# A hybrid decoder trunk on one core: rounding steps, SSD groups and GDN taps in other places

## The chip, the cores and the metric

The kernel runs on one core of a Trainium2 chip. The metric is the device time of one execution in microseconds, the median of several runs. TensorE (PE in the profile) multiplies matrices, with PEld for its weight loads; VectorE is DVE, ScalarE is ACT, GpSimd is POOL, SyncE is SP. Each engine works through its own queue of instructions in order, and the engines meet only at semaphores.

## The reference

A two-layer trunk on 256 prompt tokens and 8 x 4 sample tokens, 288 columns together, width 2048:

```python
for i in range(DEPTH):                     # DEPTH = 2
    hn = rmsnorm(h, norm_w[i])
    mix = gdn_mixer(...) if i % 2 == 0 else ssd_mixer(...)
    h = h + mix
    e = rmsnorm(p_i @ w_proj, norm_w)      # ple_add
    h = h + e * sigmoid(h @ w_gate)
y = rmsnorm(h, final_norm_w)
```

The GDN mixer (gated DeltaNet, 16 query/key heads of 128, 32 value heads) projects hn to q, k, v and z, convolves q, k, v over 4 positions, applies silu, and runs the delta rule in chunks for the prompt (with a triangular inverse per chunk) and token by token for the samples. The SSD mixer (Mamba-2, 8 groups of 8 heads of 64, state 128) projects to z, x, B, C and dt, convolves, and runs chunked state space duality for the prompt and a recurrence for the samples. Each mixer multiplies its branch with silu(z), normalises and projects back to 2048. Outputs are y and all states and convolution caches, all float32.

## The kernel before

**Precision and the weight stream.** The weights are read in halves of a tile: 128 x 1024 float32 into one of four places of `ring` by SyncE (L303 to L312). ScalarE rounds a half to `wh` (`upper`, L796 to L801; `ahead` rounds the two halves of one tile), GpSimd computes the rest `wl` = ring - wh in four instructions of 128 x 256 (`lower`, L327). The input is likewise split into `xh` (ScalarE, `split_x`, L811) and `xl` (VectorE, `lower_x`, L1345). `project` (L340) is one of eight slots of a tile of 128 output rows: two pieces of 128 inner rows, for each three matmuls with 288 columns, w_h x_h, w_h x_l and w_l x_h (L350, L351, L352). A slot is thus 6 matmuls, a tile 48. Its first slot and its fifth wait for `wl_ready`. A place of wh may be written again when TensorE has finished the half three before it (`half_done`). `project_pair` (L361) runs the first two tiles of a stage interleaved, so that each new piece of x is used at once for both.

**Stages.** The norm of x and a few GDN tiles of preparation; the GDN loop over 16 heads, the last one written out; the output projection (two `dense` parts of 16 tiles, the second fed by `split_x`); `ple` (the projection of p and the gate stage: sixteen tiles, each followed by sigmoid, a product and a sum on VectorE, and a square); the norm before SSD (`normed_x`, `norm_x`); the SSD loop over 8 groups, the last one written out; output projection and `ple` again, and the final norm.

**Mixing.** In the GDN and SSD loops TensorE's queue is written out by hand: slot e of the group's projection, then the small matmuls of the current group that hang at e (`gdn_mix`, `ssd_mix`; `gdn_ready` holds a slot's wait ahead of the projection). GDN has slots 0 to 47 a head, SSD 80 a group. ScalarE's and VectorE's orders are written out beside it: in the SSD loop `took(k)` takes tile k out of PSUM and rounds tile k + 2; `decays(c)` makes the decay matrix of chunk c from eight Relu and one Exp; `conv_silu` follows the convolution. VectorE's `do.link` makes an instruction wait for the one before it where it needs its result.

**What touches the change.** In GDN the inverse is built in six levels; at each, VectorE multiplies a result with a mask (`mask_p`, L1527), TensorE multiplies, VectorE subtracts (`less_q`, L1537, L1540). Between them lie the taps of the value convolution (`v_tap`, L1514 to L1523), and at levels 3 and 4 two sample steps (`g_bs`, L1554, and `g_es`). In SSD TensorE's groups hang at slots 21, 25, 27, 29, 31, 35, 39, 42, 46, 57 and 72: transposes at 21, the first chunk's state matmul (L717) at 25, which needs `s_xd` of VectorE's `decayed(0)` (L1812), the sample read at 27 and so on. In `ple`, ScalarE rounds `te + 1` and `te + 2` after split_x, then waits for the sum of squares, takes the root, and goes on with `gate` and `square`; VectorE follows the root with a reciprocal (L1721), sixteen scalings (L1724), and then one `gated` step for each tile (L1732, L1733), whose result `hnew` ScalarE's later gates and squares wait for.

Of the kernel before, what the change touches and what calls it, by code (L numbers as in the profile page):

```python
# [19 lines left out]
ALU = mybir.AluOpType  # L20
# [3 lines left out]
P = 128  # L24
# [58 lines left out]
G_DVE_LINKS, S_DVE_LINKS = 17, 36  # L83
# [52 lines left out]
def build(nc, weights, x_in, p_in, prm_in, cst_in, gpack, spack, gstate, sstate,  # L136
          y_out, gconv_out, sconv_out, gst_p, gst_s, sst_p, sst_s,
          g_rows, s_rows, h_spill, G_DVE, G_ACT, S_DVE, S_ACT):
    with ExitStack() as ctx:  # L139
# [199 lines left out]
        def _(pe):  # L339
# [72 lines left out]
            def gdn_ready(m, e):  # L412
# [5 lines left out]
                if e == 14:  # L418
                    pe.wait_ge(S("g_bs"), m + 1)
                if e == 26:  # L420
                    pe.wait_ge(S("g_sample_act"), m * 4 + SMP_ACT["vnds"])

            def gdn_mix(m, e, more):
# [56 lines left out]
                if e == 14:  # L480
# [35 lines left out]
                if e == 22:  # L516
# [5 lines left out]
                if e == 23:  # L522
# [9 lines left out]
                if e == 26:  # L532
# [151 lines left out]
            def ssd_mix(m, e):  # L684

                if e == 21:
# [10 lines left out]
                if e == 27:  # L697
# [8 lines left out]
                if e == 29:  # L706
# [7 lines left out]
                if e == 25:  # L714
                    pe.wait_ge(S("s_xd"), m * 2 + 1)
                    pe.wait_ge(S("s_btc"), m + 1)
                    pe.matmul(psA[:, :], sBT[:, 0, :], sa["XD"], start=True, stop=True).then_inc(S("s_s"), 1)  # L717
                for c in range(NC):
                    if e == (31, 39)[c]:
                        pe.wait_ge(S("s_w"), m * 2 + c + 1)  # L720
                        for i in range(SX):
                            for j in range(2):
                                mm = pe.matmul((psB, psC)[c][HD * j:HD * j + HD, i * P:(i + 1) * P],
                                               sX[:, c, 2 * i + j, :], sDT[:, 2 * i + j, :], start=True, stop=True)
                        mm.then_inc(S("s_y"), 1)
                if e == 35:
                    pe.wait_ge(S("s_s1"), m + 1)
                    for i in range(SX):
# [1372 lines left out]
```

## Time and profile before

| what | us |
|---|---|
| median of 3 runs | 2591.24 (2588.82 to 2592.79) |
| the profiled execution, its own time | 2590.68 |
| its span | 2588.9 |
| TensorE busy | 2439.7 (94%) |
| GpSimd busy | 1734.7 (67%) |
| VectorE busy | 1491.2 (58%) |
| ScalarE busy | 1181.6 (46%) |

The span goes from the first to the last instruction that the profiler recorded; the execution's own time is 1.8 us more. Busy times are of one execution. A matmul's duration in the timeline is longer than the distance between two starts, since matmuls overlap, so what one costs is read from the distance of starts.

### The profile page before, as it was taken

What the parts mean: (1) busy time and instruction counts of PE and PEld (TensorE: products, weight loads), DVE (VectorE), ACT (ScalarE), POOL (GpSimd) and SP (SyncE); (2) the same over time, 40 slices, a digit from 0 to 9 for tenths busy, and PEclk for the clock granted to TensorE, in tenths of its full rate; (3) what the DMA queues carried; (4) which work ended last, traced back from release to release, by engine and by line L of the source; (5) the groups of instructions that cost most, each with busy time, mean ns of one, the idle gap of its engine ahead of it and who ended that gap; (6) DMA issues with size and microseconds to landing.
All of it is one profiled execution on the core that took longest, in us unless ns stands there. A gap on an engine that the chain in (4) does not pass through costs nothing.

```text
span 2588.9 us, 58121 instructions
## 1 busy us (share of the span) xinstructions
PE 2439.7 (94%) x21088; PEld 2262.6 (87%) x21088; DVE 1491.2 (58%) x2978; ACT 1181.6 (46%) x2116; POOL 1734.7 (67%) x2236
## 2 busy tenths in 40 slices
PE   5999999999999999999998989999999999999887
PEld 4889888888888888889998879988898888899887
DVE  7555665555656556562114457888888888611434
ACT  4444444444444444443334346454545455433433
POOL 4455555555555555556797768877887777889776
PEclk9999999999999999999999989999999999999989
DMA  5344444334333343434443336655576546454433
GB/s 193 137 147 140 145 139 147 123 134 139 127 129 129 139 145 139 139 133 169 147 163 135 136 140 228 230 182 184 199 237 207 184 169 220 176 175 156 141 123 125
DMA packets 126772, 410.83 MB, mean 159 GB/s; under 512 B 21345, under 2 KB 37985, under 8 KB 122113
## 3 DMA queue, kind: packets, MB, share of 16 engines
q1 hardware_dynamic: 81216, 295.75, 33.0%
q10 hardware_dynamic: 45504, 114.38, 13.1%
q8 instruction: 35, 0.57, 0.1%
q14 instruction: 17, 0.13, 0.0%
HBM read 363.47 MB, written 46.61 MB: 158 GB/s over the span
## 4 chain that ended last, share of the span: by engine, by line
POOL 59%; issue 37%; PE 3%; POOLq 1%; DVE 0%; ACT 0%; DVEq 0%; ACTq 0%
POOL wl L327 59%; PE psj L350 1%; PE psj L352 1%; PE psj L351 1%; POOLq L331 0%; POOLq L325 0%; DVE h L1940 0%; DVE arena L1938 0%; ACT L1150 0%; POOLq L327 0%; ACT arena L1125 0%; PE psA L374 0%; ACT arena L1333 0%; DVE arena L1410 0%; DVEq L139 0%
## 5 line engine op out<-in xcount | busy, mean ns | idle before, releaser
L327 POOL TENSOR_TENSOR wl<-ring,wh 128x256 fp32r<-128x256 f32 x2232 | 1734.5, 811 | 832.5 <-ACT wh L801 829.9
L350 PE MATMUL psj<-xh,wh 128*128 128x288 f32 x4400 | 1376.3, 313 | 74.9 <-POOL wl L327 33.7
L351 PE MATMUL psj<-xl,wh 128*128 128x288 f32 x4400 | 1312.7, 298 | 0.0
L352 PE MATMUL psj<-xh,wl 128*128 128x288 f32 x4400 | 1307.5, 297 | 0.0
L350 PEld LDWEIGHTS psj<-xh,wh 128*128 128x128 f32 x4400 | 838.0, 190 | 143.7 <-issue 62.9
L351 PEld LDWEIGHTS psj<-xl,wh 128*128 128x128 f32 x4400 | 840.8, 191 | 5.4 <-issue 4.4
L352 PEld LDWEIGHTS psj<-xh,wl 128*128 128x128 f32 x4400 | 841.9, 191 | 0.0
L801 ACT ACTIVATE wh<-ring 128x1024 fp32r<-128x1024 f32 x558 | 575.2, 1056 | 530.6 <-PE psj L352 464.3
L872 ACT ACTIVATE arena<-psj 128x256 f32<-128x256 f32 x112 | 42.6, 381 | 265.9 <-PE psj L352 265.9
L1766 DVE SCALAR_TENSOR_TENSOR arena<-arena 128x256 f32<-128x256 f32 x144 | 124.2, 902 | 2.6
L1699 DVE TENSOR_TENSOR h<-h,psj 128x288 f32 x32 | 14.5, 454 | 173.7 <-PE psj L352 173.7
L1518 DVE SCALAR_TENSOR_TENSOR arena<-arena 128x256 f32<-128x256 f32 x192 | 100.4, 563 | 0.0
L1732 DVE TENSOR_TENSOR arena<-Y,arena 128x288 f32<-128x288 f32 x32 | 21.6, 674 | 120.2 <-ACT arena L1119 120.2
L1689 DVE COPY Y<-psj 128x288 f32 x22 | 10.1, 458 | 131.5 <-PE psj L352 131.5
L1439 DVE SCALAR_TENSOR_TENSOR arena<-arena 128x256 f32<-128x256 f32 x192 | 83.8, 494 | 1.2
L1527 DVE TENSOR_TENSOR arena<-psC,cst 128x256 f32<-128x256 f32 x96 | 40.6, 423 | 56.1 <-PE psC L379 54.2
L379 PEld LDWEIGHTS psC<-arena 128*64 128x64 f32 x1536 | 52.8, 138 | 15.9 <-issue 15.9
L379 PE MATMUL psC<-arena 128*64 128x64 f32 x1536 | 66.1, 228 | 0.0
L1886 DVE TENSOR_TENSOR h<-h,arena 128x512 f32<-128x512 f32 x64 | 64.9, 1013 | 0.2
L1540 DVE SCALAR_TENSOR_TENSOR arena<-psE,cst,arena 128x256 f32<-128x256 f32 x96 | 46.4, 483 | 30.8 <-PE psE L379 27.9
L1537 DVE TENSOR_TENSOR arena<-arena,psA 128x256 f32<-128x256 f32 x80 | 33.7, 422 | 51.4 <-PE psA L379 48.1
L1119 ACT ACTIVATE arena<-psj 128x288 f32<-128x288 f32 x32 | 13.1, 409 | 107.5 <-PE psj L352 107.5
(345 smaller groups left out, 2895.0 us busy)
## 6 DMA issues: line engine op xcount, KB each, us to landing
ring<-weights_d SPq DMA_DIRECT2D x558, 512.0 KB, 3.3
h<-gstate_d ACTq DMA_DIRECT2D x16, 1024.0 KB, 4.8
gst_s_d<-h ACTq DMA_DIRECT2D x16, 1024.0 KB, 4.6
h<-sstate_d ACTq DMA_DIRECT2D x32, 512.0 KB, 5.4
sst_s_d<-h ACTq DMA_DIRECT2D x32, 512.0 KB, 6.0
arena<-g_rows_d ACTq DMA_DIRECT2D x16, 864.0 KB, 4.2
arena<-s_rows_d ACTq DMA_DIRECT2D x8, 1152.0 KB, 8.0
h_spill_d<-h ACTq DMA_DIRECT2D x2, 2304.0 KB, 8.0
```

Source lines behind the costliest of these rows:

```text
L327: ins = pool.tensor_tensor(wl[:, s, n:n + 2], ring[:, s, n:n + 2], wh[:, s, n:n + 2].bitcast(F32), ALU.subtract)
L350: pe.matmul(out, w_h, xh[:, kt, :], start=(kt == 0), stop=False)
L351: pe.matmul(out, w_h, xl[:, kt, :], start=False, stop=False)
L352: mm = pe.matmul(out, w_l, xh[:, kt, :], start=False, stop=(kt == KT - 1))
L379: mm = pe.matmul(bank[r:r + 64, cols], lhsT[:, r:r + 64], rhs, start=True, stop=True)
L801: act.activation(wh[:, hc % 4], ring[:, hc % 4], ACT.Copy).then_inc(wh_ready, 1)
L872: return lambda bank: (act.activation(U[:, i, UP:UC], bank[:, 0:SEQ], ACT.Copy), act.activation(U[:, i, US:UW], bank[:, SEQ:T], ACT.Copy))[1]
L1439: ins = dve.scalar_tensor_tensor(out, src, tap(i, j), out, ALU.mult, ALU.add)
L1518: ins = dve.scalar_tensor_tensor(out, gU[:, 2 + i, at:at + b - a], gpc_tap[1][:, i, j:j + 1], out, ALU.mult, ALU.add)
L1540: dve.scalar_tensor_tensor(E, packed(psE[:, 0:2 * P], lv), cst[:, K_BM, K_ROW + lv:K_ROW + lv + 1], E, ALU.mult, ALU.add).then_inc(S("g_de ...
L1766: ins = dve.scalar_tensor_tensor(out, src, w, out, ALU.mult, ALU.add)
L1886: do.link(dve.tensor_tensor(sS[:, b], sS[:, b], bc(sEGb[:, :, b], 2, HD), ALU.mult))
```

## The change

- SyncE loads the first and third quarter of x and the constants; ScalarE loads the second and fourth quarter and prm, and no longer waits for prm before it issues the loads of gpack.
- `split_x` and `normed_x` can round one half of the next tile before their wait for `half_done`, and one in the middle of their sixteen pieces. The dense stages use both; the gate stage the one in the middle, and a half of its first tile at i = 13 of the squares. After the root ScalarE rounds tile by tile between the first gates, and the squares come two gates behind instead of one.
- SSD: groups at 20, 32, 34, 44, 49, 59 and 72 instead of eleven. The state matmul of the first chunk goes from slot 25 to 32, with the sample read; slot 34 holds the off-diagonal product, the second state, the sample transposes and the first chunk's y; slot 44 the second chunk's y and the transposes of 42. ScalarE's silu of the sample rows goes behind `decays(0)`, the copy of the first state goes before the copy of the sample read, and VectorE's steps for the second chunk go ahead of the sample steps.
- GDN: `v_tap` does either the prompt or the sample part; they stand one by one between masks and subtractions and end behind mask 4. The wait for `g_bs` goes from slot 14 to 15, the groups of 22, 26 and 28 go to 23 and 27. The cache rows `gco` are copied later with a semaphore `g_co` of their own, and the silu of the value rows comes before the DMA of the cache.

The core of the diff:

```diff
-            for n in range(4):
+            for n in (0, 2):
                 sp.dma_start(h[:, 4 * n:4 * n + 4, :], x_in[:, 4 * n:4 * n + 4, :]).then_inc(S(f"x_in{n}"), 16)
-                if n == 0:
-                    sp.dma_start(cst[:, :, :], cst_in).then_inc(c_in, 16)
-                    sp.dma_start(prm[:, :], prm_in).then_inc(S("prm_in"), 16)
+            sp.dma_start(cst[:, :, :], cst_in).then_inc(c_in, 16)
             for s in range(4):
...
-                if e == 14:
+                if e == 15:
                     pe.wait_ge(S("g_bs"), m + 1)
-                if e == 26:
+                if e == 27:
                     pe.wait_ge(S("g_sample_act"), m * 4 + SMP_ACT["vnds"])
...
-                if e == 22:
+                if e == 23:
                     pe.wait_ge(S("g_es"), m + 1)
                     pe.wait_ge(S("g_rss"), m + 1)
...
-                if e == 23:
                     pe.wait_ge(S("g_vnd"), m * 2 + 1)
...
-                if e == 26:
+                if e == 27:
+                    pe.wait_ge(S("g_rhs"), m + 1)
+                    new_values(1)
...
-                if e == 27:
-                    pe.wait_ge(S("g_rhs"), m + 1)
-                    new_values(1)
-                if e == 28 and more:
-                    gdn_norm(m + 1)
+                    if more:
+                        gdn_norm(m + 1)
                 if e == 29:
...
-                if e == 21:
+                if e == 20:
...
+                def chunk_state(c):
+                    pe.wait_ge(S("s_xd"), m * 2 + c + 1)
+                    pe.matmul(psA[:, :], sBT[:, c, :], sa["XD"], start=True, stop=True).then_inc(S("s_s"), 1)
+
+                def chunk_y(c):
+                    pe.wait_ge(S("s_w"), m * 2 + c + 1)
...
+                if e == 32:
+                    pe.wait_ge(S("s_btc"), m + 1)
+                    chunk_state(0)
                     pe.wait_ge(S("s_pr"), m + 1)
                     col_sum(psF[:, 0:NPAIR], sPR)
...
-                if e == 29:
+                if e == 34:
+                    pe.wait_ge(S("s_s1"), m + 1)
...
+                    chunk_state(1)
                     pe.wait_ge(S("s_roc"), m + 1)
...
-                if e == 25:
-                if e == 35:
...
-                    pe.wait_ge(S("s_xd"), m * 2 + 2)
-                    pe.matmul(psA[:, :], sBT[:, 1, :], sa["XD"], start=True, stop=True).then_inc(S("s_s"), 1)
-                if e == 42:
+                    chunk_y(0)
+                if e == 44:
+                    chunk_y(1)
                     pe.wait_ge(S("s_xe"), m + 1)
...
                 for r in range(2):
-                    if e == (46, 57)[r]:
+                    if e == (49, 59)[r]:
...
-            def split_x(src, n, t0):
-
+            def split_x(src, n, t0, first=False, second=False):
+
+                if first:
+                    upper(0, 0, 2 * t0 + 2)
                 if t0:
                     act.wait_ge(half_done, 2 * t0)
                 for kt in range(n):
+                    if second and kt == n // 2:
+                        upper(0, 0, 2 * t0 + 3)
                     act.activation(xh[:, kt, :], src(kt), ACT.Copy).then_inc(xh_ready, 1)
 
-            def normed_x(base, t0, t_next):
+            def normed_x(base, t0):
 
                 act.wait_ge(S("hss"), base // KT + 1)
                 act.activation(dRS, psA[:, 0:T], ACT.Sqrt, bias=eps_c, scale=1.0 / D_MODEL) \
                     .then_inc(S("n_root"), 1)
                 if t0:
+                    upper(0, 0, 2 * t0 + 2)
                     act.wait_ge(half_done, 2 * t0)
                 else:
                     ahead(0, 0, 0)
                 for kt in range(KT):
+                    if kt == 3 and not t0:
+                        upper(0, 0, 2)
                     if kt == KT // 2:
-                        ahead(0, 0, t_next)
+                        upper(0, 0, 2 * t0 + 3)
                     act.wait_ge(S("xn"), base + kt + 1)
                     act.activation(xh[:, kt, :], dTM[:, kt % 2, :], ACT.Copy).then_inc(xh_ready, 1)
...
+            for n in (1, 3):
+                act.dma_start(h[:, 4 * n:4 * n + 4, :], x_in[:, 4 * n:4 * n + 4, :]).then_inc(S(f"x_in{n}"), 16)
+            act.dma_start(prm[:, :], prm_in).then_inc(S("prm_in"), 16)
             act.wait_ge(S("konst"), 1)
             act.activation(small[:, 7:8], eps_c, ACT.Sqrt)
-            act.wait_ge(S("prm_in"), 16)
...
-            normed_x(0, 0, 1)
+            normed_x(0, 0)
             act.dma_start(h_spill, h[:, :, :]).then_inc(S("spill"), 16)
+            act.wait_ge(S("prm_in"), 16)
...
                 act.wait_ge(S("g_convv"), m + 1)
+                act.activation(gCR[:, 2:4, :], gCR[:, 2:4, :], ACT.Silu).then_inc(S("g_cv"), 1)
+                if full:
+                    g_load_v(m + 1)
+                else:
+                    split_x(lambda kt: Y[:, kt, :], KT, T_O1)
...
+                act.wait_ge(S("g_co"), m + 1)
                 act.dma_start(gconv_out[m, 1], gco[:, 2:4, :]).then_inc(S("g_cv_out"), 16)
-                if full:
-                    g_load_v(m + 1)
-                act.activation(gCR[:, 2:4, :], gCR[:, 2:4, :], ACT.Silu).then_inc(S("g_cv"), 1)
-                if not full:
-                    split_x(lambda kt: Y[:, kt, :], KT, T_O1)
                 act.wait_ge(S("g_tokv"), m + 1)
...
             def dense(t0, src):
-                split_x(src, KT, t0)
-                ahead(0, 0, t0 + 1)
+                split_x(src, KT, t0, True, True)
                 with act.Fori(0, KT // 2 - 1) as i:
                     for k in range(2):
                         ahead(i, 2, t0 + 2 + k)
...
                 for i in range(KT):
                     if i == 7:
                         ahead(0, 0, te)
+                    if i == 13:
+                        upper(0, 0, 2 * te + 2)
                     act.wait_ge(took_dve, td + i + 1)
                     act.activation(eq[:, i, :], eb[:, i, :], ACT.Square).then_inc(S("esq"), 1)
 
...
                         .then_inc(S("hsq"), 1)
 
                 act.wait_ge(took_dve, td)
-                split_x(lambda kt: h[:, kt, :], KT, te)
-                ahead(0, 0, te + 1)
+                split_x(lambda kt: h[:, kt, :], KT, te, second=True)
                 ahead(0, 0, te + 2)
                 act.wait_ge(S("ess"), hq // KT)
                 act.activation(dRE, psB[:, 0:T], ACT.Sqrt, bias=eps_c, scale=1.0 / D_MODEL) \
                     .then_inc(S("e_root"), 1)
                 gate(0, 0)
+                ahead(0, 0, te + 3)
                 gate(0, 1)
-                square(0, 0)
-                with act.Fori(0, KT // 2 - 2) as i:
+                for k in range(2):
+                    ahead(0, 0, te + 4 + k)
+                    gate(0, 2 + k)
+                    square(0, k)
+                with act.Fori(0, KT // 2 - 3) as i:
                     for k in range(2):
-                        ahead(i, 2, te + 3 + k)
-                        gate(i, 2 + k)
-                        square(i, 1 + k)
-                ahead(0, 0, te + KT - 1)
-                gate(0, KT - 2)
-                square(0, KT - 3)
+                        ahead(i, 2, te + 6 + k)
+                        gate(i, 4 + k)
+                        square(i, 2 + k)
                 if not end:
                     ahead(0, 0, te + KT)
+                gate(0, KT - 2)
+                square(0, KT - 4)
                 gate(0, KT - 1)
+                square(0, KT - 3)
...
-            normed_x(16, T_SPRO, T_SPRO + 1)
+            normed_x(16, T_SPRO)
...
-                def took(k):
+                def took(k, between=None):
 
                     tile_wait(mt, per, t0 + k)
                     bank = psj[(t0 + k) % 2]
...
                         act.activation(sZS[:, z_of[k], :], bank[:, 0:T], ACT.Silu).then_inc(took_act, 1)
                     if not full and k == SX - 1:
                         split_x(lambda kt: Y[:, kt, :], KT, T_O2)
+                    if between is not None:
+                        between()
                     ahead(mt, per, t0 + k + 2)
...
                 took(0)
                 conv_silu(m, 1)
-                took(1)
-                conv_silu(m, 2).then_inc(S("s_cv"), 1)
-                act.wait_ge(S("s_sconv"), m + 1)
-                act.activation(sCV[:, :, SEQ:T], sCV[:, :, SEQ:T], ACT.Silu).then_inc(S("s_scv"), 1)
+                took(1, lambda: conv_silu(m, 2).then_inc(S("s_cv"), 1))
...
                 act.activation(sa["DEC"], sa["DEC"], ACT.Exp).then_inc(S("s_dec"), 1)
                 decays(0)
+                act.wait_ge(S("s_sconv"), m + 1)
+                act.activation(sCV[:, :, SEQ:T], sCV[:, :, SEQ:T], ACT.Silu).then_inc(S("s_scv"), 1)
                 if full:
                     act.wait_ge(S("s_cv"), m + 1)
                     s_load_pack(m + 1)
                 took(2)
+                if not full:
+                    took(3)
+                act.wait_ge(S("s_s"), m * 2 + 1)
+                act.activation(sS1, psA[:, :], ACT.Copy).then_inc(S("s_s1"), 1)
                 act.wait_ge(S("s_ro"), m + 1)
                 act.activation(sRO, psE[:, :], ACT.Copy).then_inc(S("s_roc"), 1)
-                act.wait_ge(S("s_s"), m * 2 + 1)
-                act.activation(sS1, psA[:, :], ACT.Copy).then_inc(S("s_s1"), 1)
-                took(3)
+                if full:
+                    took(3)
                 act.wait_ge(S("s_y"), m * 2 + 1)
...
-                def v_tap(i, j):
-
...
+                def v_tap(i, j, part):
+
+                    a, b, at = ((0, SEQ, j), (SEQ, T, UC + DEC_B * j))[part]
+                    out = gCR[:, 2 + i, a:b]
+                    return dve.scalar_tensor_tensor(out, gU[:, 2 + i, at:at + b - a], gpc_tap[1][:, i, j:j + 1],
+                                                    out, ALU.mult, ALU.add)
...
+                mask_p(0)
+                do.link(v_tap(0, 0, 0))
+                less_q(0)
+                do.link(v_tap(0, 0, 1))
+                mask_p(1)
+                do.link(v_tap(1, 0, 0))
+                less_q(1)
+                v_tap(1, 0, 1)
+                do.link(v_tap(0, 1, 1))
+                mask_p(2)
+                do.link(v_tap(0, 1, 0))
+                less_q(2)
+                do.link(v_tap(1, 1, 0))
+                mask_p(3)
+                dve.wait_ge(S("g_sample_pe"), m * 6 + SMP_PE["sqs"])
...
+                do.link(v_tap(0, 2, 0))
+                less_q(3)
+                v_tap(1, 2, 0)
+                do.link(v_tap(1, 1, 1))
+                mask_p(4)
+                v_tap(0, 2, 1)
+                v_tap(1, 2, 1).then_inc(S("g_convv"), 1)
+                dve.wait_ge(S("g_sample_pe"), m * 6 + SMP_PE["esp"])
...
+                if not full:
+                    lower_x(lambda kt: Y[:, kt, :], KT, X0["oa1"])
+                less_q(4)
                 dve.tensor_copy(gco[:, 2:4, 0:PRE], gU[:, 2:4, UC - PRE:UC])
-                dve.tensor_copy(gco[:, 2:4, PRE:CW], gU[:, 2:4, UW - PRE * DEC_B:UW])
-                for lv in range(6):
-                    mask_p(lv)
-                    if lv < PRE:
-                        v_tap(0, lv)
...
+                do.link(dve.tensor_tensor(sCB[:, :, :], psD[:, 0:2 * P].rearrange("p (c t) -> p c t", c=NC),
+                                  bc(cst[:, K_INC, :], 1, NC), ALU.mult))
                 dve.wait_ge(S("s_scv"), m + 1)
...
-                dve.wait_ge(S("s_cb"), m + 1)
                 dve.wait_ge(S("s_dt"), m * 2 + 1)
                 dve.tensor_tensor(sDT[:, :, :], sDT[:, :, :], bc(sCB[:, 0, :], 1, HPG), ALU.mult).then_inc(S("s_w"), 1)
+                if last:
+                    lower_x(lambda kt: Y[:, kt, :], KT, X0["oa2"])
                 dve.wait_ge(S("s_s"), m * 2 + 1)
                 decayed(1)
 
                 dve.tensor_tensor(sXS[:, :, :], sCV[:, 2:6, SEQ:T], sRP[:, :, 192:224], ALU.mult)
+                dve.wait_ge(S("s_off"), m + 1)
+                y1 = sYT[:, :, CH:SEQ]
+                do.link(dve.tensor_tensor(y1, psD[:, :].rearrange("p (i t) -> p i t", i=SX), sRP[:, :, 32:160],
+                                          ALU.mult))
+                dve.wait_ge(S("s_s"), m * 2 + 2)
+                s1 = sS1.rearrange("p (h d) -> p h d", h=HPG)
+                do.link(dve.tensor_tensor(s1, s1, bc(sEGc, 2, HD), ALU.mult))
+                dve.tensor_tensor(sS1, sS1, psA[:, :], ALU.add).then_inc(S("s_s2"), 1)
...
-                if last:
-                    lower_x(lambda kt: Y[:, kt, :], KT, X0["oa2"])
...
```

## Rows read from the trace of the kernel before

**Rows 1.** The page's busy table, and its costliest group on GpSimd.

```profile
PE 2439.7 (94%) x21088; PEld 2262.6 (87%) x21088; DVE 1491.2 (58%) x2978; ACT 1181.6 (46%) x2116; POOL 1734.7 (67%) x2236
...
L327 POOL TENSOR_TENSOR wl<-ring,wh 128x256 fp32r<-128x256 f32 x2232 | 1734.5, 811 | 832.5 <-ACT wh L801 829.9
```

**Rows 2.** TensorE's waits: us in total, times, longest us.

```profile
PE psj L350 <- POOL wl L327: 33.7, 8, 6.3
...
PE psA L717 <- DVE arena L1812: 18.2, 7, 2.6
...
PE psA L379 <- DVE arena L1527: 3.2, 14, 0.2
```

**Rows 3.** Windows: stretch, us, busy by engine, PEclk, DMA share, GB/s.

```profile
1300.00:1380.00 80.00, 80.00 (x602) 80.00 (x601) 13.67 (x25) 26.49 (x26) 73.14 (x103) 1.00 0.49 171
1288.00:1293.00 5.00, 5.00 (x23) 5.00 (x23) 0.00 (x0) 0.00 (x0) 4.96 (x8) 0.50 0.61 208
```

**Rows 4.** Timeline, one GDN head: start us, us, engine, line, [idle before].

```profile
388.29 0.40 PE L350 MATMUL psj<-xh,wh 128*128 128x288 f32 x1 [0.64 <-DVE arena L1554]
...
411.70 0.40 PE L350 MATMUL psj<-xh,wh 128*128 128x288 f32 x1
...
412.59 0.61 PE L508 MATMUL psC<-arena 128*128 128x128 f32 x4
```

**Rows 5.** Timeline, TensorE at the stages' first waits for wl.

```profile
1287.52 0.61 PE L350 MATMUL psj<-xh,wh 128*128 128x288 f32 x1 [4.21 <-POOL wl L327]
...
1416.66 0.61 PE L350 MATMUL psj<-xh,wh 128*128 128x288 f32 x1 [5.83 <-POOL wl L327]
...
1440.39 0.61 PE L350 MATMUL psj<-xh,wh 128*128 128x288 f32 x1 [6.28 <-POOL wl L327]
```

**Rows 6.** Windows at half clock behind the six waits, first and sum.

```profile
1286.40:1293.20 6.80, 5.68 (x23) 5.68 (x24) 0.00 (x0) 0.00 (x0) 6.61 (x10) 0.50 0.45 154
...
sum 34.00, PE 25.03 PEld 25.04 DVE 4.28 ACT 6.19 POOL 33.14; mean PE 4.17 PEld 4.17 DVE 0.71 ACT 1.03 POOL 5.52
```

**Rows 7.** Timeline, first gate stage, VectorE and GpSimd.

```profile
1425.64 1.95 DVE L1721 RECIPROCAL arena<-arena 128x288 f32<-128x288 f32 x1 [10.29 <-ACT arena L1133]
1427.62 6.96 DVE L1724 SCALAR_TENSOR_TENSOR Y<-Y,prm,arena 128x288 f32<-128x288 f32 x16
...
1437.06 11.89 POOL L327 TENSOR_TENSOR wl<-ring,wh 128x256 fp32r<-128x256 f32 x16 [10.03 <-ACT wh L801]
```

**Rows 8.** Timeline, VectorE in the norm before SSD.

```profile
1545.76 0.87 DVE L1358 SCALAR_TENSOR_TENSOR arena<-h,prm,arena 128x288 f32<-128x288 f32 x1
1546.55 0.99 DVE L1364 TENSOR_TENSOR xl<-arena,xh 128x288 fp32r<-128x288 f32 x1
...
1549.42 0.52 DVE L1358 SCALAR_TENSOR_TENSOR arena<-h,prm,arena 128x288 f32<-128x288 f32 x1
1549.86 0.45 DVE L1364 TENSOR_TENSOR xl<-arena,xh 128x288 fp32r<-128x288 f32 x1
```

**Rows 9.** Timeline, an SSD group (TensorE, ScalarE) and the last one's end.

```profile
1692.24 0.37 ACT L1264 ACTIVATE arena<-psA 128x256 f32<-128x256 f32 x1
1692.63 1.28 ACT L1266 ACT_TABLE_LOAD   x1
...
1693.91 1.13 PE L717 MATMUL psA<-arena 128*128 128x512 f32 x2 [2.60 <-DVE arena L1812]
...
1694.55 2.43 ACT L1244 ACTIVATE arena<-arena 128x128 f32<-128x128 f32 x8
1697.02 1.06 ACT L1248 ACTIVATE arena<-arena 128x1024 f32<-128x1024 f32 x1
...
2208.91 0.58 PE L350 MATMUL psj<-xh,wh 128*128 128x288 f32 x1 [4.03 <-DVE xl L1349]
```

**Rows 10.** The start: ScalarE's first squares, and x's four transfers.

```profile
7.53 1.11 ACT L865 ACTIVATE arena<-h 128x288 f32<-128x288 f32 x3 [5.28 <-DMA prm<-prm_in_d]
...
DMA to landing us min/median/max: 3.9/6.7/8.2
```

More of the change, by code:

```diff
@@ L479, in gdn_mix @@
                     mm.then_inc(S("g_sample_pe"), 1)
-                if e == 14:
+                if e == 15:
                     for j in range(2):
@@ L696, in ssd_mix @@
                     mm.then_inc(S("s_tok"), 1)
-                if e == 27:
+                def chunk_state(c):
[3 more added lines that the diff above has]
+                    pe.wait_ge(S("s_w"), m * 2 + c + 1)
+                    for i in range(SX):
+                        for j in range(2):
+                            mm = pe.matmul((psB, psC)[c][HD * j:HD * j + HD, i * P:(i + 1) * P],
+                                           sX[:, c, 2 * i + j, :], sDT[:, 2 * i + j, :], start=True, stop=True)
+                    mm.then_inc(S("s_y"), 1)
+                if e == 32:
+                    pe.wait_ge(S("s_btc"), m + 1)
+                    chunk_state(0)
                     pe.wait_ge(S("s_pr"), m + 1)
@@ L705, in ssd_mix @@
                     mm.then_inc(S("s_ro"), 1)
-                if e == 29:
+                if e == 34:
+                    pe.wait_ge(S("s_s1"), m + 1)
+                    for i in range(SX):
+                        mm = pe.matmul(psD[:, i * P:(i + 1) * P], sS1[:, i * P:(i + 1) * P],
+                                       sCV[:, 1, CH:2 * CH], start=True, stop=True)
+                    mm.then_inc(S("s_off"), 1)
+                    chunk_state(1)
                     pe.wait_ge(S("s_roc"), m + 1)
@@ L713, in ssd_mix @@
                     mm.then_inc(S("s_smp"), 1)
-                if e == 25:
[L715 to L725, printed above, removed]
-                if e == 35:
-                    pe.wait_ge(S("s_s1"), m + 1)
-                    for i in range(SX):
-                        mm = pe.matmul(psD[:, i * P:(i + 1) * P], sS1[:, i * P:(i + 1) * P],
-                                       sCV[:, 1, CH:2 * CH], start=True, stop=True)
-                    mm.then_inc(S("s_off"), 1)
-                    pe.wait_ge(S("s_xd"), m * 2 + 2)
-                    pe.matmul(psA[:, :], sBT[:, 1, :], sa["XD"], start=True, stop=True).then_inc(S("s_s"), 1)
-                if e == 42:
+                    chunk_y(0)
+                if e == 44:
+                    chunk_y(1)
                     pe.wait_ge(S("s_xe"), m + 1)
@@ L1512, in gdn_body @@
                 ins.then_inc(S("g_mk"), 1)
-                def v_tap(i, j):
-                    for a, b, at in ((0, SEQ, j), (SEQ, T, UC + DEC_B * j)):
-                        out = gCR[:, 2 + i, a:b]
-                        ins = dve.scalar_tensor_tensor(out, gU[:, 2 + i, at:at + b - a], gpc_tap[1][:, i, j:j + 1],
-                                                       out, ALU.mult, ALU.add)
-                    if (i, j) == (1, PRE - 1):
-                        ins.then_inc(S("g_convv"), 1)
-                    else:
-                        do.link(ins)
+                def v_tap(i, j, part):
[3 more added lines that the diff above has]
+                                                    out, ALU.mult, ALU.add)
                 def mask_p(lv):
@@ new lines, in gdn_body @@
+                dve.tensor_tensor(gBS[:, :, :], bc(ident[0:NS, 0:NS], 1, 2),
+                                  psD[0:NS, 256:256 + 2 * NS].rearrange("p (j t) -> p j t", j=2), ALU.add) \
+                    .then_inc(S("g_bs"), 1)
+                do.link(v_tap(0, 2, 0))
[6 more added lines that the diff above has]
+                dve.wait_ge(S("g_sample_pe"), m * 6 + SMP_PE["esp"])
@@ L1568, in qk_taps @@
+                mask_p(5)
+                less_q(5)
                 def qk_taps(js):
```

34 lines of the change are left out of this document (6 added, 28 removed).

## Prediction

> **What bounds the kernel now.** I read the busy table of the page first: TensorE is busy 94% of the span. GpSimd, busy 67%, is named often as the one that others wait for, but of its own 832.5 idle us 829.9 end with ScalarE's rounding [rows 1]: it is a link between ScalarE and TensorE, not the bound. So TensorE's own queue sets the end, and time can come from four things only: waits in it, half clock, the step from projections to group work and back, and less work. The arithmetic stays the same.
>
> Next I read TensorE's waits [rows 2]. 33.7 us in 8 waits are for wl, up to 6.3 us each; they stand at the begin of the output stages. 18.2 us are seven waits of L717 for DVE L1812 in the SSD loop; 3.2 us are fourteen of L379 for L1527 in the GDN loop.
>
> Last I read the price of a projection matmul: in 80 us of a dense stage 602 start, 0.133 us each, at the granted clock 1.00 (2.4 GHz); in 5 us behind a wait 23 start, 0.22 to 0.24 us each, at 0.50 (1.2 GHz) [rows 3]. A long wait is paid twice.
>
> **GDN loop (16 heads).** (a) The wait for g_bs (L1554) before slot 14's projection is 0.64 us [rows 4]; at slot 15, a slot of about 0.9 us later, g_bs is there. (b) Today two taps run between a mask and the subtraction behind it, or the other way, and TensorE waits for it: 3.2/14 = 0.23 us per head [rows 2], and as much again, an estimate, in the projection run that starts inside the same lateness. A piece alone fits under a projection slot. I take 0.4 us. (c) Three group slots disappear (22, 26, 28). A run of six projection matmuls between two groups takes 0.89 us (411.70 to 412.59) instead of 6 x 0.133 = 0.80 [rows 3, 4]; I take 0.1 to 0.2 each, 0.12, so 0.36. Sum 1.4 us, times 15 = 21.0; bounds 1.0 and 1.8 per head, 15 to 27. New waits: ScalarE waits for the silu of the value rows until their taps end, now behind mask 4, and for g_co; behind the last it has only g_tokv's work, which comes later. In the last head, where split_x of the output stage stands behind that silu, I book 0.4 us won. Sum 21.4.
>
> **Output stages (dense, twice).** ScalarE today makes sixteen xh pieces and only then rounds the next half; GpSimd's four subtractions end 4.21 us too late for TensorE [rows 5]. With one half rounded before the wait and one in the middle, wl is there. What is late next is xh piece 8, behind the rounding in the middle, and DVE's xl pieces, slowed by GpSimd: 0.5 us. Gain 2 x (4.21 - 0.5) = 7.4; bounds 5 and 8.4.
>
> **Gate stages (twice).** The waits are 5.83 and 6.28 us, and the same in the second layer, 24.2 in all [rows 5]. What comes instead, each time: the square behind the early rounding, 0.4; xl pieces beside GpSimd, 0.8; e_sum's wait for DVE's sums, 0.3. Then the second wait does not go entirely. ScalarE's gate(0, 2) waits for the first new h, and that follows DVE's sixteen scalings, 6.96 us today, 0.44 each, with GpSimd idle for 10.03 us around them [rows 7]. GpSimd will now work through all of them. The nearest rows are DVE's in the norm before SSD, beside GpSimd and without it: the scaling L1358 takes 0.87 against 0.52, the subtraction L1364 0.99 against 0.45 [rows 8]. At 0.8 us each, sixteen are 12.8 us, so the first new h comes some 15 us behind the root (reciprocal 1.95), while TensorE has three tiles of 48 x 0.133 = 6.4 us, of which the root takes the first part: I work out 3.2 us of wait before the fifth tile. At the end a third square stands behind the last gate: 0.5. Gain 24.2 - 2 x (0.4 + 0.8 + 0.3 + 3.2 + 0.5) = 13.8; bounds 4 (scalings at 1.1) and 22 (at 0.45).
>
> **Half clock behind these six waits.** TensorE works 25.03 us at 0.50 behind them [rows 6], each matmul at 0.24 instead of 0.133: 11.1 us are lost. All of it goes but 1.1 us for each new wait in the gate stages: 8.9; bounds 6 and 11. Output and gate stages together: 7.4 + 13.8 + 8.9 = 30.1.
>
> The Trainium skill (SBUF — State Buffer, SBUF: two separate sides) speaks against this step: an instruction of VectorE with two SBUF inputs and one of GpSimd exclude each other for whole instructions. By it every scaling would wait out one GpSimd instruction of 0.7 us, 16 x 1.15 = 18.4 us, and each gate stage would lose another 5.6. The rows agree that they slow each other, by a factor of 1.7 to 2.2.
>
> **SSD loop (8 groups).** DVE's chain is continuous up to L1812, so slot 25's state matmul waits 2.60 us in the iterations from the second on [rows 9]. In slot 32 its input is long there. Gone per iteration: 2.60; four group slots, 0.5; what the wait costs in the clock behind it, 0.9 (an estimate from [rows 6]: 4.2 us at half clock, of which 1.9 are lost, follow each wait of 4 to 6 us); small waits at L709 and L723 together, 0.9, an estimate. 4.9 us. But slots 21 to 31 hold no group now, and TensorE is at slot 32, the first of tile 4, after eleven slots of 0.80 us, 8.9 us behind the transposes. Tile 4's weights are rounded by took(2), and this stays behind decays(0) in ScalarE's order and now also behind the sample silu. Its chain from the transposes: copy 0.35, table load 1.28, three exps 0.6, decays 2.43 + 1.06 [rows 9], then a second table load 1.28, silu 0.4, take_u 0.45, rounding 1.0, GpSimd's four 2.8, and 0.6 for handing over: 12.2 us. New wait: 3.3 us in every iteration, also in the first. Today TensorE comes there 5 us later and nobody waits. 4.9 - 3.3 = 1.6; six times 9.8, the first one 2.3 lost, half clock 1 lost. Sum 6.5; bounds -8 (also 2.2 us at slot 44 if DVE's linked sample steps run at their speed beside GpSimd) and 30 (no new wait). The last group: today 2.6 [rows 2] and 4.03 us of waits [rows 9] and one between them; 2.5 of half clock (by [rows 6]). Then 3.3 at slot 32, 0.6 for its xl, and 2.1 at slot 34, where the second state waits behind sixteen xl pieces. Gain 4.8; bounds 0 and 9.
>
> **Norm before SSD.** ScalarE rounds in two single steps and one earlier, so less of norm_x runs beside GpSimd at the upper prices of [rows 8]: 1.5 us; bounds 0 and 3.
>
> **Start.** The squares start at 7.53, ended by prm's landing; x's four transfers land 3.9 to 8.2 us after their issues [rows 10], so a quarter takes 1.43 us and the first was there at 0.8 + 3.9 = 4.7. Over two queues the first two quarters land together at about 6.1, so 1.4 us are won. The third half begun at piece 3 keeps TensorE busy sooner: 1.6. Sum 3.0; bounds 1 and 5. ScalarE's three DMA issues ahead of its table load, and the gpack issues behind it, lie under the wait for x.
>
> **Sum.** 21.4 + 30.1 + 6.5 + 4.8 + 1.5 + 3.0 = 67.3 us. The profiled execution took 2590.68, 1.8 us more than its span and 0.6 less than the median of the runs; 2590.7 - 67.3 = 2523.4, and I predict 2523.
>
> **Rivals.** *No new wait at slot 32* (0.12): ScalarE's chain is shorter than I add up, or TensorE comes later. Speaks for it that GpSimd is idle there; against it the order of ScalarE's queue. 8 x 3.3 = 26 less: 2497. *Earlier rounding only moves the wait* (0.15): the slowdown between GpSimd and DVE gives the stages' gain back, the scalings take 1.15 us each and the xl pieces in the dense stages run out too: 30.1 becomes 13: 2540. *The finer taps miss* (0.06): another DVE instruction is late in the inversion and (b) and part of (a) come back, 0.8 x 16: 2536. *Slower than before* (0.05): slot 32's wait is worse. ScalarE's rounding of tile 4 is now behind s_sconv, the end of DVE's sample convolution; each us that this comes later than ScalarE asks for it is one of TensorE's wait, eight times. It decides at a wait of 3.3 + 67/8 = 11.7 us: 2592 and more. *The edits do little* because other waits stand behind each: 0.02, 2589. My forecast has 0.60.
>
> **Numbers.** The bounds' half widths, added as squares, give about 14 us around the forecast; reaching to the rivals on both sides: 2498 to 2550. Faster by over 0.2% (5 us, about what a measurement of this kernel can tell from no change): 0.93; within: 0.02; slower: 0.05.
>
> **What would show it.** GDN: no wait for L1554, a head's period 1.4 us shorter. Dense: the 4.2 us waits for wl under 0.6, no half clock there. Gate: the first wait gone, a second of 2 to 4 us released by ScalarE's gate or the first new h, DVE's scalings at 0.7 to 0.9 us. SSD: no wait at L717, one of 3 us for wl at L350, a second table load before took(2). Start: squares from about 6. The prediction is wrong if the wait at slot 32 is absent or grows past 5 us, or if the scalings keep 0.44 us.

## Result and profile after

The changed kernel takes 2576.56 us (median of five runs; 2574.27 to 2577.94), the kernel before 2591.24 (also of five): a ratio of 0.9944, 95% interval 0.993 to 0.9959. It is faster by 0.56%, 14.7 us, where 68 us were forecast and 2550 was the end of the range.

I split both traces at the first projection matmul of each stage. A positive number is time won by the stage; the sum is the difference of the two spans, 2588.9 and 2575.0.

| stage | forecast us | measured us |
|---|---|---|
| start and first tiles | 3.0 | 1.7 |
| GDN loop and last head | 21.4 | 20.0 |
| output stages, both | 11.4 | 9.3 |
| gate stages, both | 18.7 | 12.6 |
| norm before SSD | 1.5 | 0.6 |
| SSD loop, groups 1 to 7 | 6.5 | -21.7 |
| last SSD group, to the second dense stage | 4.8 | -8.5 |

(The gate row is -1.31 for the projection of p and 6.24 for the gate tiles in the first layer, -1.39 and 9.06 in the second, the last with the final norm in it.) Outside SSD the gate stages are 6.1 us off, no other stage more than 2.1. "Last SSD group" runs from its first tile through the first half of the output projection. The SSD edits lost 30.2 us: the section from the loop's first tile to the second dense stage was 735.3 us and is 765.5.

The busy table and GpSimd's group of the changed kernel, against [rows 1]:

```profile
PE 2450.3 (95%) x21088; PEld 2267.1 (88%) x21088; DVE 1465.1 (57%) x2978; ACT 1199.8 (47%) x2130; POOL 1761.8 (68%) x2236
...
L325 POOL TENSOR_TENSOR wl<-ring,wh 128x256 fp32r<-128x256 f32 x2232 | 1761.6, 822 | 787.9 <-ACT wh L800 785.3
```

TensorE does the same 21088 matmuls, but is busy for 10.6 us longer, and its mean granted clock is 0.974 where it was 0.980: that is the first hint that the loss is not in waits alone. ScalarE has fourteen instructions more, all table loads: eight ahead of the sample silu, and seven more ahead of the Exp of `decays(1)`, less one elsewhere.

TensorE's waits after (us in total, times, longest), against [rows 2]:

```profile
PE psj L348 <- POOL wl L325: 32.5, 10, 4.5
...
PE psj L348 <- ACT arena L1130: 6.9, 2, 3.7
...
PE psA L696 <- DVE arena L1841: 3.2, 1, 3.2
```

The sum for wl has hardly changed, 32.5 for 33.7, and this is a trap: the waits are other ones. The four of the gate stages and two of the dense stages [rows 5] are gone; eight in SSD's slot 32 stand in their place, one a group, and two short ones are left. L717's seven waits are gone as well, as are those for L1554 and L1527.

Slot 32 of the second SSD group in the changed kernel, TensorE's timeline and then ScalarE's:

```profile
1675.93 0.61 PE L348 MATMUL psj<-xh,wh 128*128 128x288 f32 x1 [3.83 <-POOL wl L325]
...
1677.54 1.91 PE L696 MATMUL psA<-arena 128*128 128x512 f32 x2
1679.24 0.56 PE L372 MATMUL psF<-arena,cst 128*128 128x80 f32 x2
```

```profile
1668.15 1.06 ACT L1264 ACTIVATE arena<-arena 128x1024 f32<-128x1024 f32 x1
1668.29 0.34 ACTq L1195 DMA_DIRECT2D arena<-spack_d  x1
1669.23 1.28 ACT L1285 ACT_TABLE_LOAD   x1
1670.52 0.37 ACT L1285 ACTIVATE arena<-arena 128x192 f32<-128x192 f32 x1
1670.80 0.36 ACT L881 ACTIVATE arena<-psj 128x256 f32<-128x256 f32 x1
1671.07 0.19 ACT L882 ACTIVATE arena<-psj 128x32 f32<-128x32 f32 x1
1671.14 2.00 ACT L800 ACTIVATE wh<-ring 128x1024 fp32r<-128x1024 f32 x2
```

This is the chain that I added up: decays, table load, silu, take_u, rounding. TensorE stopped at 1672.1 and went on at 1675.93. What I had not added stands behind it: from the start of L696's two matmuls to that of L372 it is 1.70 us.

Windows of the changed kernel at half clock around slot 32 of the eight SSD groups (columns as in [rows 3]; first two, last and sum):

```profile
1589.50:1596.30 6.80, 5.95 (x22) 3.21 (x26) 0.90 (x2) 0.60 (x1) 3.54 (x6) 0.50 0.46 154
1674.80:1681.60 6.80, 5.67 (x22) 3.18 (x26) 0.89 (x2) 0.60 (x1) 3.82 (x6) 0.50 0.45 154
...
2186.80:2193.60 6.80, 4.78 (x18) 2.97 (x22) 6.80 (x9) 6.53 (x16) 6.76 (x9) 0.50 0.25 85
sum 54.60, PE 43.91 PEld 24.58 DVE 13.06 ACT 10.71 POOL 34.27; mean PE 5.49 PEld 3.07 DVE 1.63 ACT 1.34 POOL 4.28
```

TensorE works 43.91 us at 1.2 GHz there, and the last group has more behind it: the granted clock is 0.50 again from 2200.5 to 2210.7. Before, the 2.60 us waits were followed by half clock in four of seven groups, for 13.05 us of work in all:

```profile
1777.90:1781.30 3.40, 3.40 (x18) 2.96 (x20) 0.51 (x2) 3.37 (x11) 0.00 (x0) 0.50 0.09 22
...
sum 13.60, PE 13.05 PEld 10.40 DVE 4.19 ACT 13.48 POOL 0.00; mean PE 3.26 PEld 2.60 DVE 1.05 ACT 3.37 POOL 0.00
```

### The profile page after: what moved, and what is told of

It is laid out like the page before. It is cut to its first block, busy times and chain, and to the rows that moved or that the text cites. A ratio compares the mean times of both kernels' runs of the same rounds, so it can differ in the third digit from the quotient of the medians.

```text
span 2575.0 us, 58133 instructions
## 1 busy us (share of the span) xinstructions
PE 2450.3 (95%) x21088; PEld 2267.1 (88%) x21088; DVE 1465.1 (57%) x2978; ACT 1199.8 (47%) x2130; POOL 1761.8 (68%) x2236
## 4 chain that ended last, share of the span: by engine, by line
POOL 49%; issue 32%; PE 14%; DVE 3%; ACT 1%; POOLq 1%; ACTq 0%; DVEq 0%
POOL wl L325 49%; PE psj L348 5%; PE psj L350 4%; PE psj L349 4%; DVE xl L1367 1%; DVE Y L1753 1%; POOLq L329 0%; DVE h L1968 0%; POOLq L323 0%; DVE h L1914 0%; ACT wh L800 0%; PE psA L696 0%; PE psA L747 0%; PE psj L659 0%; ACT xh L819 0%
## 5 line engine op out<-in xcount | busy, mean ns | idle before, releaser
L325 POOL TENSOR_TENSOR wl<-ring,wh 128x256 fp32r<-128x256 f32 x2232 | 1761.6, 822 | 787.9 <-ACT wh L800 785.3
L348 PE MATMUL psj<-xh,wh 128*128 128x288 f32 x4400 | 1365.1, 310 | 75.1 <-POOL wl L325 32.5
L1795 DVE SCALAR_TENSOR_TENSOR arena<-arena 128x256 f32<-128x256 f32 x144 | 123.6, 897 | 2.6
L1728 DVE TENSOR_TENSOR h<-h,psj 128x288 f32 x32 | 14.5, 454 | 154.9 <-PE psj L350 154.9
L1428 DVE TENSOR_TENSOR arena<-arena 128x288 f32<-128x288 f32 x45 | 22.8, 506 | 109.3 <-ACT arena L1136 101.9
L1457 DVE SCALAR_TENSOR_TENSOR arena<-arena 128x256 f32<-128x256 f32 x192 | 83.7, 494 | 1.2
L1536 DVE SCALAR_TENSOR_TENSOR arena<-arena 128x256 f32<-128x256 f32 (+1 forms) x192 | 69.0, 381 | 0.0
L1551 DVE TENSOR_TENSOR arena<-arena,psA 128x256 f32<-128x256 f32 x80 | 33.7, 421 | 62.1 <-PE psA L377 62.1
L1554 DVE SCALAR_TENSOR_TENSOR arena<-psE,cst,arena 128x256 f32<-128x256 f32 x96 | 46.5, 484 | 31.4 <-PE psE L377 27.8
L377 PE MATMUL psE<-arena 128*64 128x64 f32 x1536 | 61.9, 223 | 0.0
```

The lines of the kernel that those rows point to most:

```text
L325: ins = pool.tensor_tensor(wl[:, s, n:n + 2], ring[:, s, n:n + 2], wh[:, s, n:n + 2].bitcast(F32), ALU.subtract)
L348: pe.matmul(out, w_h, xh[:, kt, :], start=(kt == 0), stop=False)
L377: mm = pe.matmul(bank[r:r + 64, cols], lhsT[:, r:r + 64], rhs, start=True, stop=True)
L1457: ins = dve.scalar_tensor_tensor(out, src, tap(i, j), out, ALU.mult, ALU.add)
L1536: return dve.scalar_tensor_tensor(out, gU[:, 2 + i, at:at + b - a], gpc_tap[1][:, i, j:j + 1], out, ALU.mult, ALU.add)
L1554: dve.scalar_tensor_tensor(E, packed(psE[:, 0:2 * P], lv), cst[:, K_BM, K_ROW + lv:K_ROW + lv + 1], E, ALU.mult, ALU.add).then_inc(S("g_de ...
```

## Experiments

Ratios are to the kernel before, with 95% intervals. What a run gains against the changed kernel is the difference of the two medians.

**The change without its SSD part, and the SSD part alone.** In the first the groups, ScalarE's order and VectorE's order of the SSD loop are those of before; in the second they alone are new.

> The changed kernel with TensorE's groups, ScalarE's and VectorE's order of the SSD loop as before (s_cb stays a link, for the number of semaphores). Theory: the SSD edits cost what the section from the loop's first tile to the second dense stage shows, 765.5 against 735.3 us, so 30 us come back: 2546 us, a loop period of 83.1 and again a 2.6 us wait at the first state matmul. Rival (the rest of the change lengthens the SSD section through its changed start, the roundings in took or the norm): 2565 or more, and a loop period that stays near 85.

> The kernel before with the SSD edits alone. Theory: 30 us slower than before, 2621 us, a wait for wl of 3.8 us in slot 32 in all eight groups, a loop period of 85.4. Rival (the loss is an interaction with the other edits): within 10 us of before.

2547.37 us, 0.9833 (0.9816 to 0.9849), and 2619.19 us, 1.0112 (1.0095 to 1.0129). By themselves the SSD edits cost 28 us (30 were expected), taken out they give 29 back. They are additive to the rest, so the cause is inside them. In the second run the waits for wl double in number:

```profile
PE psj L350 <- POOL wl L327: 65.1, 16, 6.3
```

**Tile 4 rounded early.**

```diff
                 act.activation(sa["BT"], psA[:, 0:2 * P], ACT.Copy).then_inc(S("s_btc"), 1)
+                ahead(mt, per, t0 + 4)
+                act.wait_ge(S("s_sconv"), m + 1)
+                act.activation(sCV[:, :, SEQ:T], sCV[:, :, SEQ:T], ACT.Silu).then_inc(S("s_scv"), 1)
+                took(2, rounded=True)
...
                 decays(0)
-                act.wait_ge(S("s_sconv"), m + 1)
-                act.activation(sCV[:, :, SEQ:T], sCV[:, :, SEQ:T], ACT.Silu).then_inc(S("s_scv"), 1)
...
-                took(2)
```

> The changed kernel, with ScalarE's two roundings of tile 4 ahead of the sample silu, the exps and decays(0), and the silu ahead of the exps (one table load fewer). Theory (the loss is ScalarE's order: 3.8 us of wait and 2.5 us of half clock on the float32 group matmuls behind it): no wait for wl in slot 32, the two state and read groups at 0.85 and 1.7 instead of 1.7 and 2.7 us, loop period 79 to 80, 2526 to 2535 us. Rival (the merged groups ask too early for VectorE's work anyway): a wait for s_pr or s_w of 2 to 4 us takes its place, period above 83, above 2555 us.

2522.75 us, 0.9736 (0.9719 to 0.9752): 54 us less than the changed kernel and 3 less than the range expected, with the same groups on TensorE. The edit moves more than the two roundings: the silu and take_u of tile 2 go ahead of the exps too, and one table load of each group falls away. A group takes 78.7 to 79.5 us; it was 82.8 to 83.3 before and is 85.3 to 85.5 in the changed kernel. The same matmuls in this run:

```profile
1665.50 1.02 PE L696 MATMUL psA<-arena 128*128 128x512 f32 x2
1667.06 0.45 PE L372 MATMUL psF<-arena,cst 128*128 128x80 f32 x2 [0.54 <-DVE arena L1860]
```

and two groups later:

```profile
1824.47 1.02 PE L696 MATMUL psA<-arena 128*128 128x512 f32 x2
1825.33 0.34 PE L372 MATMUL psF<-arena,cst 128*128 128x80 f32 x2
```

The wait for wl is gone, and from the start of L696 to that of L372 it is 0.86 us, not 1.70, in the five groups without a wait between them. So the merged groups, fed in time, win 4.4 us a group on average, close to the 4.9 that I had summed; ScalarE's order took it away. The rival, that the merged groups ask too early for VectorE's work, shows as 0.54 us in two groups, each 0.8 us longer than the others. The section of the last group is not mended: 160.0 us, where the kernel before took 157.7; a wait of 4.55 us for the first xl pieces stands there.

**The roundings between decays and silu.** Here only `ahead(mt, per, t0 + 4)` moves, to a place ahead of the second table load, so that short waits stay.

> The changed kernel with only the order of two ScalarE steps in the SSD loop turned round: decays(0), then the two roundings of tile 4, then the second table load with the sample silu, where the silu stood first. It shortens the 3.83 us wait in slot 32 by the 1.95 us of table load and silu and keeps it as a wait. The silu is 2 us later, so VectorE's s_pr is late for the same slot by 1 to 1.5 us. Theory (each long wait brings 3 us of half clock in the float32 group matmuls behind it, and short ones do not): clock back in most groups, period 81.5 to 82.5, 2545 to 2556 us. Rival (the loss is the wait's own length and nothing else): the gain is only what the waits lose, 8 x 0.5 to 8 x 1.9, 2561 to 2572 us.

2544.61 us, 0.9822 (0.9807 to 0.9837). Its waits:

```profile
PE psF L372 <- DVE arena L1860: 8.8, 7, 1.3
PE psj L348 <- ACT arena L882: 8.8, 8, 1.2
```

(L882 is the second copy of take_u, which empties the PSUM bank that the projection of slot 32 writes; it now comes behind the silu.) The window at the same place:

```profile
1666.40:1673.20 6.80, 5.54 (x36) 3.20 (x37) 5.06 (x8) 1.85 (x5) 2.50 (x4) 1.00 0.43 154
```

The waits of a group are 1.17 + 1.26 = 2.43 us, 1.40 less than 3.83, but its period is 81.64, 3.72 less than 85.36. The other 2.3 us are the clock: it stays at 1.00 through both waits of all seven groups, and TensorE starts 36 matmuls in 6.8 us where it was 22. The rival (only the wait counts) gave 2561 to 2572 and is out.

**Four scalings ahead.**

```diff
-                for i in range(KT):
-                    ins = dve.scalar_tensor_tensor(eb[:, i, :], eb[:, i, :], prm[:, wc + i:wc + i + 1], dRE,
-                                                   ALU.mult, ALU.mult)
-                do.link(ins)
+                scaled(0, 4)
...
                 gated(0, 0)
                 gated(0, 1)
+                scaled(4, KT)
```

> The changed kernel, with four of VectorE's sixteen scalings in each gate stage ahead of the first two gated steps and twelve behind them. Theory (the 3.68 us wait for ScalarE's gate comes from the sixteen scalings of 0.92 us beside GpSimd): the wait and the 2.3 us of half clock behind it go in both stages, 11 to 12 us: 2565 us. Rival (the first wait at the stage, for xl, takes it up, or the later h costs the same in another gate): under 4 us, 2573 or more.

2565.31 us, 0.9906 (0.9889 to 0.9922), 11.3 us less than the changed kernel. L1130 has left TensorE's waits: its two, 3.68 + 3.26 = 6.94 us in the changed kernel, are gone. The other 4 us I put down to the clock: of the four stretches of the gate stages at 0.50, one is left. In the changed kernel VectorE, GpSimd and TensorE show what it was:

```profile
1396.50 14.55 DVE L1753 SCALAR_TENSOR_TENSOR Y<-Y,prm,arena 128x288 f32<-128x288 f32 x16
...
1397.22 14.40 POOL L325 TENSOR_TENSOR wl<-ring,wh 128x256 fp32r<-128x256 f32 x16 [0.18 <-ACT wh L800]
...
1413.07 0.60 PE L348 MATMUL psj<-xh,wh 128*128 128x288 f32 x1 [3.68 <-ACT arena L1130]
```

Sixteen scalings in 14.55 us, 0.91 each against 0.44 with GpSimd idle [rows 7]. In this run four of them take 2.78 us and the first new h is there at 1402.1, not at 1412.4.

**The xl pieces of the last group in two parts.** Six ahead of `decayed(1)`, ten behind it.

> The changed kernel with one edit in the last SSD group: VectorE makes six of the output projection's sixteen xl pieces ahead of decayed(1) and ten behind it. Theory (the second state in slot 34 waits 3.21 us because all sixteen pieces, 13.99 us at 0.87 each, stand ahead of it): no wait there, 3 to 4 us off the section, 2573 us. Rival (VectorE is the bound of that whole section, so a later wait for take_out's copies grows by as much): section unchanged within 1 us, 2576 us.

2567.92 us, 0.9907 (0.9893 to 0.9921), 8.6 us less than the changed kernel; the section itself gains 6.1, where 3 to 4 were expected. VectorE in the changed kernel, and in this run:

```profile
2186.26 13.99 DVE L1367 TENSOR_TENSOR xl<-Y,xh 128x288 fp32r<-128x288 f32 x16
```

```profile
2185.81 5.49 DVE L1367 TENSOR_TENSOR xl<-Y,xh 128x288 fp32r<-128x288 f32 x6
2191.90 0.69 DVE L1841 TENSOR_TENSOR arena<-arena 128x512 f32<-128x512 f32 x1 [0.59 <-PE psA L696]
2192.51 8.06 DVE L1367 TENSOR_TENSOR xl<-Y,xh 128x288 fp32r<-128x288 f32 x10
```

The 3.21 us wait of L696 is gone; a wait of 1.46 us comes at the second y group (L702), so the rival is right in part. The rest of the 6.1 is clock again: behind the 3.21 us wait the changed kernel worked at half clock, here it does not. The spans of the two profiled executions differ by 6.7 us; what the medians have beyond that lies within their intervals, and I leave it open.

**The GDN part in two.** VectorE's and ScalarE's half alone, and TensorE's half alone.

> The kernel before with VectorE's and ScalarE's part of the GDN edits alone (taps in pieces, g_co, silu ahead of the DMA); TensorE's groups and waits as before. By the prediction's terms: 0.4 us a head from the pieces, the 0.64 us wait for g_bs stays: period 68.9, 2585 us. Rival (the finer taps miss): period 69.3, 2591 us.

> The kernel before with TensorE's part of the GDN edits alone: g_bs at slot 15, groups of 22, 26 and 28 merged. By the prediction's terms: 0.64 and 0.36 us a head, period 68.3, 2576 us. If merging saves nothing: period 68.7, 2581 us.

2583.53 us, 0.9972 (0.9961 to 0.9984), and 2577.34 us, 0.9948 (0.9933 to 0.9963). A head takes 69.34 us before, 68.87 with the taps, 68.61 to 68.65 with the slots, and 68.17 with both. So the taps give 0.47 (forecast 0.4) and the slots 0.71 (forecast 1.0); together they are additive. The 0.71 is the wait for g_bs alone: slots 13 to 15 take 5.54 us for 6.23, while slots 22 and 23 (3.23 before and after) and 26 to 29 (6.98 and 6.99), where the groups were merged, take what they took. The 0.36 us booked for three group slots fewer did not come.

**The edits together.**

> The changed kernel with both edits of the two runs before: tile 4 rounded early, and four scalings ahead of the first gated steps. If the two act on different waits their gains add up: 2522.75 - (2576.6 - 2565.3) = 2511.5 us. If one of them used cover of the other: 2516 or more.

> The changed kernel with all three edits: tile 4 rounded early, four scalings ahead, the xl pieces in two parts. In the run with the first two the second state of the last group waited for nothing (its slot comes later there, behind a 4.55 us wait for the first xl pieces), so the third edit has no wait to remove: 2513 to 2515 us. If it adds its 6 to 8 us all the same: 2507.

2513.74 us, 0.9702 (0.9689 to 0.9715), and 2515.4 us, 0.9707 (0.9694 to 0.972). The first two edits act on different waits and nearly add up: the second still gives 9.0 of its 11.3 us. The third has nothing to take away once tile 4 is early: 2513.74 is the best version, 3% under the kernel before. In the profiled execution with all three, the rival of the run with tile 4 early has grown:

```profile
PE psF L372 <- DVE arena L1864: 3.1, 6, 0.5
```

Six of the first seven groups wait about 0.52 us for VectorE and take 79.5 us instead of 78.7; with two edits one group did. Why the number of such groups differs from run to run is not shown.

## Why the prediction was wrong

**The step that failed is the term for half clock in the SSD loop, "half clock 1 lost".** The new wait itself was forecast at 3.3 us in every group, for the right reason, and measured at 3.83, 4.47 in the last group. I booked 1 us of half clock for the seven groups of the loop. A group costs 85.36 - 78.68 = 6.7 us more than with tile 4 early; 3.83 is the wait. Of the 2.85 that are left, 2.69 lie in slot 32, where the granted clock is 0.50; I put them down to the clock. (A few tenths may be the waits themselves: in the run with the roundings between decays and silu the clock stays at 1.00, and 2.43 us of waits lengthen the group by 81.64 - 78.68 = 2.96.) Over seven groups 2.85 make 20 us where I had 1. The whole forecast is 53 us off; 28.2 of them lie in these seven groups, 13.3 in the last one, 6.1 in the gate stages. [Rows 6] had the price: 25.03 us at half clock behind six waits of 4 to 6 us, of which 11.1 were lost, so 1.9 a wait. By them alone eight new waits would have cost 15 us. The rest is how long TensorE works at half clock behind each: 25.03 / 6 = 4.2 us there, 43.91 / 8 = 5.5 here. There these were projection matmuls, here mostly the group's state and read matmuls with 512 columns, which had been moved to slot 32, and they take twice as long as well (1.70 for 0.86).

The Trainium skill (TensorE: Matmul & The Clock Gate, HAM oscillation) describes a loop in which a wait in every round lets the clock fall again, so that the fall is paid each time. The rows of eight SSD groups agree: 0.50 in each of the eight, and 1.00 in the run with two waits of 1.2 us.

**The other SSD terms.** Gone: forecast 4.9 us a group, measured 4.4. The two small waits at L709 and L723, which I booked at 0.9 in every group, were there in two of seven only. The first group lost 8.1 us where I had 2.3: it has no wait of its own to lose, the full new one with its clock, and another of 0.73 for wl. The last group is 13.3 us off: 4.47 instead of 3.3 at slot 32; 3.21 instead of 2.1 at slot 34, since I took an xl piece at less than the 0.87 that it takes beside GpSimd; half clock behind both, not costed; and 4.6 us of waits for take_out's copies (L1484) against 1.6 before. This last cost I had not seen. I read it as VectorE being late behind the sixteen pieces, but no run shows it: with the pieces in two parts these waits are 5.0 us.

**The range.** The half widths of the bounds, added as squares, give 23 us and not the 14 that I wrote; 2576 lies outside that too. It lies even above 2568, the sum with every term at its lower bound, because the SSD loop's -8 and the last group's 0 had at most 1 us for half clock behind the new waits in them. And none of the signs that I had named for a wrong prediction appeared: the wait at slot 32 is there and under 5 us, and the scalings do not keep 0.44.

**Gate stages: the waits right, the clock wrong in the same way.** The wait for gate(0, 2) was forecast at 3.2 us and is 3.68 and 3.26; its mechanism is shown by the run with four scalings. The scalings take 0.91 us, not 0.8. The waits lost are 24.2 and 2 x 2.10 for the first xl; what stands instead is 3.44 + 3.68 + 3.52 + 3.26 (for xl and for the gate, in each layer), so 14.5 are won (forecast 13.8). But the half clock did not go. Windows of the changed kernel, both gate stages:

```profile
1381.30:1384.70 3.40, 3.37 (x14) 3.40 (x15) 3.40 (x10) 3.40 (x9) 1.47 (x1) 0.50 0.46 154
1412.00:1418.80 6.80, 5.73 (x24) 5.74 (x25) 4.59 (x8) 3.26 (x6) 4.50 (x6) 0.50 0.25 88
...
sum 20.40, PE 18.59 PEld 18.66 DVE 16.53 ACT 13.65 POOL 12.79; mean PE 4.65 PEld 4.66 DVE 4.13 ACT 3.41 POOL 3.20
```

18.59 us of TensorE's work at half clock, where the four windows of before had 2.84 + 3.01 + 5.58 + 4.52 = 15.95. Half the waiting, and more half clock: what I booked as won, 7.1 - 2.2 = 4.9 us, did not come. By the rule of the Trainium skill (SBUF — State Buffer, SBUF: two separate sides), as the prediction applied it, a scaling would have taken 1.15 us; it took 0.91, so the measurement decides against the full price; GpSimd's subtractions beside it took 0.90 instead of 0.74 [rows 7].

**What held.** GDN (1.17 us a head for 1.4, by the wait and the taps, not by the merging; no wait for L1554), the dense stages (no wait for wl and no half clock; the waits for the first xl pieces grew by 0.2 and 0.3), the norm within 1 us, and the start: the squares begin at 6.09. Of the rivals, none came as written. The nearest is the one called slower than before, for which I asked for a wait of 11.7 us in slot 32; it needed much less, since each microsecond of wait brought 0.75 of half clock with it. With the SSD edits alone it is what happened. That rival was priced by its wait only, and so its chance was too low.

## What to carry to other kernels

When a change trades one wait for another, sum both in two parts: the wait, and what half clock adds to the work behind it. Here two waits of 1.2 us cost a group 3.0, and one of 3.8 cost 6.7. When groups of work on TensorE are moved to a boundary of tiles, read in the same step what the engine that feeds this boundary does just before it, and move that first. Here two roundings moved ahead of a table load and a silu were worth 32 us; moved ahead of the decays, with the silu and one table load fewer, it was 54, nearly four times the change itself. What the roundings alone would give in that earlier place was not run.

## What the hardware showed

The clock fell while TensorE waited (it stopped at 1672.1, the granted clock was 0.50 from 1674.8) and stayed there through 5.67 us of nearly unbroken work, to 1681.6. The seven waits of 2.60 us before had no such uniform result: half clock followed four of them, twice only about 1 us after the wait's end; in the run without the SSD part it followed three of seven such waits. Two waits of 1.17 and 1.26 us, 3 us apart, never brought it in seven groups. Nor did every wait of 3.4 us: behind the one for xl in the first gate stage the granted clock was 0.50 in the changed kernel (3.44 us) and 1.00 in the run with four scalings (3.45 us).

An instruction of VectorE on 128x288 with two SBUF inputs takes 0.44 to 0.45 us alone, and 0.87 to 0.91 in a long row beside GpSimd's 128x256 subtractions. That is twice the time, and this held for the scalings as for the xl pieces. The subtractions take 0.90 in that row (16 in 14.40 us) and 0.74 in the gate stage of before (16 in 11.89 us).
